# Expert blocks by quarters with VectorE block transposes and six weight transfers, in a hybrid SSD and mixture-of-experts layer

## What is computed

```python
logits = (xt @ router_w + router_b)
top_vals, top_idx = lax.top_k(logits, 4)
gates = softmax(top_vals)
# for every expert e, on the tokens that chose it:
gu  = xb @ w_gate_up[e] + b_gate_up[e]            # 1024 -> 2048
glu = minimum(gu[:, :1024], 7.0)
lin = clip(gu[:, 1024:], -7.0, 7.0)
act = glu * sigmoid(1.702 * glu) * (lin + 1.0)
y   = (act @ w_down[e] + b_down[e]) * gate        # 1024 -> 1024
out[token] += y
```

## Time and profile before

| | us |
|---|---|
| timed runs, median of 3 | 1688.03 (1685.74 to 1691.02) |
| profiled execution | 1686.66 |
| its span, first to last instruction | 1685.1 |
| PE busy | 1593.7 (95%) |
| DVE busy | 530.4 (31%) |
| ACT busy | 399.5 (24%) |
| POOL busy | 123.4 (7%) |
| bytes read from device memory | 470.4 MB |

### The profile page before, as it was taken

One profiled execution on the slowest core, in us unless ns is written; L12 is line 12 of the kernel. 1 busy time (PEld: TensorE's weight loads), 2 busy tenths in 40 slices (PEclk: granted clock), 3 DMA queues, 4 the chain that ended last, 5 costly groups with the idle time before them and its releaser, 6 DMA issues.

```text
span 1685.1 us, 42907 instructions
## 1 busy us (share of the span) xinstructions
PE 1593.7 (95%) x18227; PEld 1166.3 (69%) x18227; DVE 530.4 (31%) x893; ACT 399.5 (24%) x587; POOL 123.4 (7%) x211
## 2 busy tenths in 40 slices
PE   6898999999994999999999999999999999999992
PEld 4897888874443776777677776777677776777660
DVE  5666888863222111111211121111211121111117
ACT  5443333341121111211221111211221111211221
POOL 1000000000032000000000000000000000000000
PEclk9997999999995999999999999999999999999995
DMA  3222222334262999999999999999999999999926
GB/s 112 90 78 82 101 100 100 149 149 184 84 202 84 375 384 370 384 385 383 382 376 376 379 388 376 382 380 393 367 387 378 382 382 378 390 382 385 374 96 255
DMA packets 75288, 479.59 MB, mean 285 GB/s; under 512 B 12128, under 2 KB 12576, under 8 KB 21122
## 3 DMA queue, kind: packets, MB, share of 16 engines
q1 hardware_dynamic: 66258, 461.65, 71.2%
q0 software_dynamic: 9008, 17.65, 3.4%
HBM read 470.40 MB, written 17.37 MB: 289 GB/s over the span
## 4 chain that ended last, share of the span: by engine, by line
PE 66%; DVE 1%; issue 1%; DMA 0%; POOL 0%; ACT 0%; POOLq 0%; SPq 0%; DVEq 0%
PE bank L1433 21%; PE bank L1439 19%; PE bank L1455 13%; PE bank L1458 7%; PE bank L1471 2%; PE bank L1479 2%; PE bank L1410 2%; PE bank L1504 1%; DVE reg_b L1161 1%; DVE reg_x L1161 0%; DMA moe_f<-n_scratch,idx_next 0%; POOL slot_table L504 0%; DVE reg_x L1178 0%; DVE reg_b L1178 0%; DMA reg_x<-in_b_down 0%
## 5 line engine op out<-in xcount | busy, mean ns | idle before, releaser
L1439 PE MATMUL bank<-ring,moe_f 128*32 128x256 f32 (+1 forms) x4096 | 679.2, 327 | 0.0
L1433 PE MATMUL bank<-ring,moe_f 128*32 128x384 f32 x6144 | 675.0, 488 | 0.0
L1439 PEld LDWEIGHTS bank<-ring,moe_f 128*32 128x32 f32 x4096 | 444.2, 110 | 94.7 <-issue 0.5
L1458 PE MATMUL bank<-ring,moe_f 128*32 128x256 f32 x1536 | 343.5, 380 | 0.0
L1455 PE MATMUL bank<-ring,moe_f 128*32 128x512 f32 (+1 forms) x3072 | 343.1, 487 | 0.0
L1131 DVE TENSOR_SCALAR moe_f<-bank 128x384 f32<-128x384 f32 x64 | 35.7, 558 | 899.2 <-PE bank L1439 899.2
L1433 PEld LDWEIGHTS bank<-ring,moe_f 128*32 128x32 f32 x6144 | 246.6, 110 | 39.6 <-issue 14.0
L1191 PE MATMUL bank<-n_hi,w_hi 128*128 128x264 f32 (+2 forms) x640 | 199.5, 312 | 7.2 <-DVE w_lo L782 6.6
L1458 PEld LDWEIGHTS bank<-ring,moe_f 128*32 128x32 f32 x1536 | 163.7, 110 | 54.2
L1191 PE MATMUL bank<-n_lo,w_hi 128*128 128x264 f32 (+2 forms) x640 | 196.6, 307 | 0.0
L1191 PE MATMUL bank<-n_hi,w_lo 128*128 128x264 f32 (+2 forms) x640 | 196.3, 307 | 0.0
(11 more groups left out here) (229 smaller groups left out, 1188.9 us busy)
## 6 DMA issues: line engine op xcount, KB each, us to landing
ring<-in_moe SPq DMA_DIRECT2D x384, 1024.0 KB, 7.1
ring<-in_w_in SPq DMA_DIRECT2D x24, 1024.0 KB, 4.9
ring<-in_w_out SPq DMA_DIRECT2D x10, 1024.0 KB, 4.9
ring<-acs_scratch SPq DMA_DIRECT2D x4, 1024.0 KB, 6.7
ring<-expert_rows SPq DMA_DIRECT2D x4, 1024.0 KB, 6.7
ring<-expert_rows SPq DMA_DIRECT2D x2, 2048.0 KB, 14.0
reg_vcs<-in_xT SPq DMA_DIRECT2D x4, 528.0 KB, 6.9
reg_x<-in_xrow SPq DMA_DIRECT2D x4, 512.0 KB, 6.1
```

The lines of the kernel that those rows point to most:

```text
L1433: mm(bank[t * LANE:(t + 1) * LANE, 2 * h + k, 0:OWN], xT[:, c, t * LANE:(t + 1) * LANE], w[:, k * OWN:(k + 1) * OWN], start=False, stop=la ...
L1439: ins = mm(out[:, :, lo - k * BANK_FF:hi - k * BANK_FF], xT[:, c, t * LANE:(t + 1) * LANE], shared[:, :, lo - t * SHARED:hi - t * SHARED], ...
L1458: ins = mm(bank[3 * LANE:, 4 + k, t % 2 * Y_SHARED:(t % 2 + 1) * Y_SHARED], act(t), w[:, Y_OWN:], start=first and t != 1, stop=last, skip_ ...
```

## The change

The expert part is laid out another way.

- Lanes: lane l now takes quarter l (256 columns) of every chunk, for all 96 tokens, in three groups of 32 (`lanes` on PE). All matmuls are 256 columns wide, 12 per chunk. The weights are reordered on the host to match, also along the contraction dimension.
- x is gathered with token parts on all 128 partitions: three gathers, each of 128 rows of 1 KB (a quarter of a token's row per lane). The result is scattered the same way, three times 128 rows of 1 KB. The table's 96 rows are read by four small loads, one per lane, and POOL adds the lane's number to them.
- The transposes of x and of gate and up are VectorE block transposes (32x32 blocks); those on PE are gone, and so are their copies.
- The biases aren't matmuls. DVE adds them in the clips, block by block of 32 columns, with the bias as a scalar per partition taken at an address from a register (`bias_col`): four instructions of 128x96 for gate and four for up, per half. The split of the biases ahead of the loop is gone; they are loaded once, 256 KB.
- y is evicted by one copy, at the end of its own block, and scattered in the same turn of POOL's loop.
- Weights move in six transfers of 2 MB per block, 16 KB per partition. SP waits until both pieces of a pair have been used; PE waits once per pair.

The diff, cut to its core:

```diff
@@ sync
             def pieces(j, e):
-                for q in range(PIECES):
+                for q in range(0, PIECES, 2):
                     hold(piece_used, j * PIECES + (q + 2 - PIECES))
-                    sp.dma_start(slot(q), moe_d[ds(e, 1), q].rearrange("o p w -> (o p) w")).then_inc(w_in[q], 16)
+                    sp.dma_start(two_slots(q), moe_d[ds(e, 1), q // 2].rearrange("o p w -> (o p) w")).then_inc(w_in[q], 16)
...
@@ gpsimd
+            def list_rows(base):
+                for l in range(LANES):
+                    pool.dma_start(idx_raw[l * LANE:(l + 1) * LANE, :],
+                                   table_d[ds(base, BLOCK), :].rearrange("(r g) t -> r (g t)", g=GRANULES)).then_inc(idx_in, 16)
+            def lane_rows():
+                return g.tensor_tensor(idx_next[:, :], idx_raw[:, :], lane_off[:, :], ALU.add)
             def gather():
-                g.indirect_dma_start(out=xg[0:BLOCK, :], out_offset=None, in_=n2_d,
...
+                for n in range(GRANULES):
+                    g.indirect_dma_start(out=xg[:, n, :], out_offset=None, in_=n2_parts,
...
             with pool.Fori(0, n_blocks) as j:
                 base = pool.value_load(blocks[0:1, ds(2 * j + 2, 1)], min_val=0, max_val=EXPERTS * CAPACITY - BLOCK)
-                pool.dma_start(idx_next[0:BLOCK, :], table_d[ds(base, BLOCK), :]).then_inc(idx_in, 16)
-                hold((idx_in, j * 16 + 32), (xtr_done, j + 1))
+                list_rows(base)
+                hold((idx_in, j * (16 * LANES) + 32 * LANES))
+                lane_rows().then_inc(idx_moved, 1)
+                hold((idx_moved, j * 2 + 3), (xT_ready, j + 1))
                 gather()
                 hold((y_ready, j + 1))
                 scatter()
-                hold((y_out, j * 16 + 16), (x_in, j * 16 + 32))
+                hold((y_out, j * (16 * GRANULES) + 16 * GRANULES), (x_in, j * (16 * GRANULES) + 32 * GRANULES))
                 pool.sem_inc(y_room, 1)
...
@@ scalar
             with act.Fori(0, n_blocks) as j:
-                y_evict(j + 1)
                 for h in range(2):
                     act.wait_ge(glu_ready, j * 2 + h + 1)
                     a.activation(sig, glu, ACT.Sigmoid, scale=ALPHA).then_inc(sig_ready, 1)
...
+                act.wait_ge(piece_used, j * PIECES + PIECES)
+                act.wait_ge(y_room, j + 1)
+                a.copy(y_sb.rearrange("p g x -> p (g x)"), bank[:, 4:6, :].rearrange("p a b -> p (a b)")[:, 0:GRANULES * QUARTER]
+                       ).then_inc(y_ready, 1)
+                act.sem_inc(y_free_moe, 1)
...
@@ vector
+                    v.transpose(glu.rearrange("p b (g r) -> p g b r", g=GRANULES), gate).then_inc(gate_raw, 1)
+                    dve.wait_ge(gate_raw, j * 2 + h + 1)
+                    for b in range(FF_BLOCKS):
+                        ins = v.tensor_scalar(glu[:, b, :], glu[:, b, :], bias_col(0, b), LIMIT, ALU.add, ALU.min)
+                    ins.then_inc(glu_ready, 1)
+                    v.transpose(up.rearrange("p b (g r) -> p g b r", g=GRANULES), lin).then_inc(gu_free, 1)
                     dve.wait_ge(gu_free, j * 2 + h + 3)
-                    steps.done(v.scalar_tensor_tensor(lin, lin, 1.0, glu, ALU.add, ALU.mult))
+                    for b in range(FF_BLOCKS):
+                        ins = v.tensor_scalar(up[:, b, :], up[:, b, :], bias_col(1, b), 1.0 - LIMIT, ALU.add, ALU.max)
+                    ins.then_inc(up_ready, 1)
+                    dve.wait_ge(up_ready, j * 2 + h + 1)
+                    dve.wait_ge(glu_ready, j * 2 + h + 1)
+                    v.scalar_tensor_tensor(up, up, 1.0 + LIMIT, glu, ALU.min, ALU.mult).then_inc(lin_ready, 1)
...
                 swiglu(0)
                 swiglu(1)
                 x_transposed(j + 2)
...
@@ tensor
+                def lanes(b, x, at, w, first, last):
+                    out = bank[:, b:b + 2, :].rearrange("p a b -> p (a b)")
+                    for g in range(GRANULES):
+                        for l in range(LANES):
+                            ins = mm(out[l * LANE:(l + 1) * LANE, g * QUARTER:(g + 1) * QUARTER],
+                                     x[:, at, g * LANE:(g + 1) * LANE], w[:, l * QUARTER:(l + 1) * QUARTER],
+                                     start=first and g != 1, stop=last, skip_group_check=True)
+                    return ins
...
+                pe.wait_ge(xT_ready, j + 1)
+                pe.wait_ge(gu_free, j * 2 + 1)
+                for q in range(4):
+                    piece(q)
                 pe.wait_ge(gu_free, j * 2 + 2)
-                for b in range(4):
-                    mm(bank[:, b, 0:OWN], sel[:, :], bias_r[:, b * OWN:(b + 1) * OWN], start=True, stop=False,
-                       skip_group_check=True)
-                for q in range(6):
+                for q in range(4, GU):
                     piece(q)
...
+                pe.wait_ge(y_free_moe, j + 1)
+                pe.wait_ge(act_ready, j * 2 + 1)
                 piece(8)
                 piece(9)
+                pe.wait_ge(act_ready, j * 2 + 2)
                 piece(10)
                 piece(11)
```

More of the change, by code:

```diff
@@ L387, in _ @@
                 wout(r, WOUT_SLOT[r])
[L388 to L389 removed]
             sp.wait_ge(tile_done, TD_C + KC)
[L391 to L392 removed]
+            for q in range(SLOTS, PIECES, 2):
+                sp.dma_start(two_slots(q), moe_d[0, q // 2]).then_inc(w_in[q], 16)
             for m in range(TT):
@@ L403, in _ @@
                             wout(n, n)
-                        else:
-                            q = n % SLOTS
-                            sp.dma_start(slot(q), moe_d[0, q]).then_inc(w_in[q], 16)
+                        elif n % 2:
+                            q = (n - 1) % SLOTS
+                            sp.dma_start(two_slots(q), moe_d[0, q // 2]).then_inc(w_in[q], 16)
+            sp.dma_start(bias, bgu_d).then_inc(bias_in, 16)
             sp.wait_ge(list_ready, 1)
@@ new lines, in scatter @@
+            def scatter():
+                for n in range(GRANULES):
+                    g.indirect_dma_start(out=yk_parts, in_=y_sb[:, n, :], in_offset=None,
+                                         out_offset=bass.IndirectOffsetOnAxis(
+                                             ap=idx_now[:, 2 * n + 1:2 * n + 2].bitcast(U32), axis=0),
+                                         bounds_check=TOPK * SEQ * LANES - 1, oob_is_err=False).then_inc(y_out, 16)
+            list_rows(0)
+            pool.wait_ge(lane_ready, LANES)
@@ L1106, in _ @@
             dve.sem_inc(gm_ready, 1)
-            def choose_bias(e):
-                v.tensor_scalar(sel[:, :], sel_lane[:, :], sel_of[:, ds(e, 1)], None, ALU.mult).then_inc(sel_ready, 1)
             def x_transposed(n):
-                dve.wait_ge(xtr_done, n)
-                for half in (1, 0):
-                    v.tensor_copy(xT[:, 4 * half:4 * half + 4, :].rearrange("p c t -> p (c t)"),
-                                  bank[:, 6 + half, 0:4 * BLOCK]).then_inc(xT_ready, 1)
+                dve.wait_ge(x_in, n * (16 * GRANULES))
+                v.transpose(xT.rearrange("p b (g r) -> p g b r", g=GRANULES),
+                            xg.rearrange("p g (b r) -> p g b r", r=LANE)).then_inc(xT_ready, 1)
             dve.sem_inc(gu_free, 2)
-            steps.settled()
-            choose_bias(0)
+            dve.wait_ge(bias_in, 16)
+            up_bias = bias.rearrange("p (n k b) -> p n k b", k=2, b=FF_BLOCKS)[:, :, 1, :]
+            v.tensor_scalar(up_bias, up_bias, 1.0, None, ALU.add).then_inc(bias_ready, 1)
             x_transposed(1)
+            dve.wait_ge(bias_ready, 1)
             dve.wait_ge(list_in, 16)
@@ L1136, in swiglu @@
                     dve.wait_ge(sig_ready, j * 2 + h + 1)
-                    v.tensor_tensor(actv, lin, sig, ALU.mult).then_inc(act_ready, 1)
+                    v.tensor_tensor(act_h[h], up, sig, ALU.mult).then_inc(act_ready, 1)
                 swiglu(0)
-                e = dve.value_load(blocks[0:1, ds(2 * j + 3, 1)], min_val=0, max_val=EXPERTS - 1)
-                choose_bias(e)
                 swiglu(1)
                 x_transposed(j + 2)
-                steps.leave(n_blocks)
             for m in range(TT):
@@ L1460, in down @@
                     return ins
                 def piece(q):
-                    pe.wait_ge(w_in[q], j * 16 + 16 * (HELD[q] + 1))
+                    if q % 2 == 0:
+                        pe.wait_ge(w_in[q], j * 16 + 16 * (HELD[q] + 1))
                     for u in range(2):
-                        ins = gate_up(q, u) if q < GU else down(q, u)
-                    ins.then_inc(piece_used, 1)
-                def act_transposes(h):
-                    pe.wait_ge(act_ready, j * 2 + h + 1)
-                    for c in range(3):
-                        ins = nc.tensor.transpose(bank[:, 6 + h, c * P:(c + 1) * P],
-                                                  actv.rearrange("p a f -> p (a f)")[:, c * P:(c + 1) * P], ident[:, :])
```

(10 more changed lines are left out.)

228 lines of the change are left out of this document (61 added, 167 removed).

## The result

The change made the kernel slower: 1710.98 us (median of four runs, 1706.48 to 1712.27) against 1687.51 us (1685.74 to 1691.02), a ratio of 1.0132 with a 95% interval of 1.0107 to 1.0156. Forecast was 1651 us.

The account below looks back on a forecast made before the run. PE's order bounds the loop; after the change the largest of POOL's round (33.2 us a block), DMA (32.8) and PE (31.9) counts. 1686.7 - 40 + 2.3 + 0.5 = 1649.5, on the median's footing 1651 us; range 1590 to 1770.

Parts of the forecast that it names:

- PE per block, and the clips: Expert block on PE: streams 30.96 us, 3.50 us of changeovers gone, clip stall 0 to 1.9, middle 0.9: 31.9 us.
- DMA load: Expert block's transfers: weights 29.5 us at 426 GB/s plus 3.3 for POOL's small packets, 32.8 us (31.2 to 36.3).
- POOL's round: Expert loop, y's copy through scatter, lists, gather to transposed x: sets the period at 33.2 us, bounds 31.0 to 35.7.
- C = 33.5 us ... I take 34.5: Length C of POOL's round: terms sum to 33.5 us, 39.5 if small packets cost like 4 KB ones; 34.5 taken.
- P = (B + C) / 2: Block period P: round C must fit in two periods less PE's own part B; (31.9 + 34.5) / 2 = 33.2 us.
- That rival: Slower: POOL's small packets stand behind 16 KB weight rows in the DMA engines; C = 45, P = 38.45, 1819 us; chance 0.26.
- the case that I gave 0.26: Slower rival, small packets behind 16 KB rows in POOL's round: holds all times from 1693 us up; chance 0.26.
- B's kinder value: B is PE's own part of a block in the period formula; the forecast took 31.9 us.
- Ahead of the loop: Before the expert loop: more list loads, offsets and gathers, less for transposes, copies and bias matmuls; net +2.3 us.
- Behind it: After the loop: fewer eviction copies, two more scatter issues, reads of y start 1.4 us later; +0.5 us, up to +1.4.
- The signs I named: At a block's start, PE waiting for DVE's x transpose means the round, for weights the load; before piece 10, the clips.
- the slow case: Slower rival, small packets behind 16 KB rows; signs: period over 34.5 us; a gather landing after 14 us or more; chance 0.26.

Follow-up runs that it names:

- the lists ahead: The changed kernel, six 2 MB transfers kept, with POOL's four list loads for a block issued one turn earlier, ahead of the wait for y: 1582.45 us, ratio 0.9383.

## Why the prediction was wrong

*PE per block, and the clips.* Right in mechanism, and better than the 31.9 us I took: a block that doesn't wait is 31.08 us. The 3.50 us of changeovers are gone, the form of rows 3 is kept up for all chunks, and the clips never make PE wait. DVE's chain in the kernel after:

```profile
1006.72 0.58 DVE L1106 STREAM_TRANSPOSE moe_f<-bank 128x384 f32<-128x384 f32 x1 [14.51 <-PE bank L1400]
1007.48 0.81 DVE L1109 TENSOR_SCALAR moe_f<-moe_f 128x96 f32<-128x96 f32 x4 [0.17 <-DVE moe_f L1106]
...
1010.38 0.56 DVE L1121 TENSOR_TENSOR moe_f<-moe_f 128x384 f32<-128x384 f32 x1
```

1006.72 to 1010.94 is 4.2 us, against 5.15 us of cover. The 0.28 us of register issue per clip that I feared is not paid: four clips are done in 0.81 us.

*DMA load.* Mis-sized, without consequence: 32.8 us was too much, 31.3 is what 419 GB/s with all of POOL's traffic give. I had asked whether small packets cost the weights' rate; over the 29.5 us of the weights alone they add 1.8 us, close to the 1.7 us that I had put for their bytes. I had also read the engines' share of 0.99 at 381 GB/s as nearly full. It was no sign of it: the share is 1.02 at 393 GB/s in the kernel with 4 KB rows, where nobody waits for weights, and 1.01 at 419 with the lists ahead.

The 358 GB/s that the Trainium skill gives for a core's loads ("DMA: Bandwidth & Descriptors", "Where 436 GB/s comes from") is passed by 17% here, with one core running.

*POOL's round.* This is the step that failed, "C = 33.5 us ... I take 34.5". The mechanism was right: the round decides, and P = (B + C) / 2 holds. From the mean of 35.25 less the clock's 1.22, P = 34.03, so C = 2 x 34.03 - 31.08 = 37.0 us. It was the landings that I took from rows 6, which are those beside packets of 8 KB, for a kernel with packets of 16 KB. Term by term, mine against the median round after: scatter 9.1 and 10.6, lists with add 8.4 and 9.9, gather 10.6 and 11.1. With 8 KB rows they are 8.8, 8.2 and 9.0, less than mine: no price for four times as many small packets is seen beyond their issue, and the row length costs 1.8, 1.7 and 2.1 us, 5.5 us in all. I had seen this and put it in a rival, with 10.5 us for it and 6 for the packets. That rival had the mechanism (the experiments show it) and twice its price; it gave 1819 us. The measured 1711 us lies in the case that I gave 0.26, and inside my range of 1590 to 1770 us; the middle of the forecast, faster by 37 us, had the wrong sign.

As to how: "DMA: Bandwidth & Descriptors", "Queues, rings and completion order", of the Trainium skill says that each DMA engine takes turns between its queues packet by packet; its packet is a bundle of several descriptors, while a packet of the profile here is one row. A small packet would then wait for one bundle of large rows each turn, and longer by the length of the rows. The round agrees from 8 to 16 KB, and does not from 4 to 8 KB, where it stays at 30.8 us. No run shows the turns themselves, so how the row lengthens the landing is argued; that it does is shown.

*The missing term.* No step of the prediction had PE's clock in it, in the sum or in a rival. With C = 37.0 alone the period would by the same sum be 34.03 us, still under the 34.46 us of before, and the kernel at 1711 - 38 = 1673 us would be faster than before by 0.8%. The 2.5 us of half clock behind each of 15 stalls turn this to 1.3% slower. So the 60 us between forecast and result are: +26 us for the round (0.83 us x 31, B's kinder value included), +38 us for the clock, and -4 us for both ends.

*Ahead of the loop.* I had +2.3; from the end of the slot table's writes to the first weight matmul it is 14.6 us against 14.7. The gather's last part lands 2.75 us behind its issue, not 4.1, and so pays for the two issues more. The 1.5 us come from the table's writes, which end 1.4 us sooner (521.53 against 522.92 us); why is not shown. *Behind it*, +0.2 us where I had +0.5.

*The signs I named.* PE waited for DVE's x transpose and for nothing else: the round, as I had put it. The landing of 14 us that I gave as the mark of the slow case was far too high a mark; 8.4 in place of 6 us is enough when three of them stand in a row.

## What to carry to other kernels

Where a chain of small DMAs decides a period, price its landings by the packets that will run beside it, not by those of today; and look at the row length of the bulk transfer, not at its size: 2 MB in rows of 8 KB cost what 1 MB in rows of 8 KB did. A gain in rate from larger rows and transfers (415 to 419 GB/s here, 8 us, of which 2.3 are ahead of the first copy of y) is only to be had once the small chain is off the critical path, so move the chain first (lists a turn earlier: 1582 us from 1711). And add to a forecast stall of PE of the lengths seen here (3 to 7 us) the half clock behind it, 1.6 to 2.5 us: around break-even that decides the sign.

## What the runs showed that I had not expected

- One transfer of 64 neighbouring partitions in 16 KB rows: 230 GB/s, with the DMA engines' share at 1.01, where 128 partitions give 419. With the even and the odd 64 in turn PE no longer waited for weights, at the 369 GB/s that its blocks asked for.
- With PE asking for 421 GB/s, 1 MB pieces in 8 KB rows got 415 and 2 MB pieces in 16 KB rows 419. 4 KB rows carried the 393 that were asked of them.
- On one chip PE ran at half pace, at full granted clock, around the third issue of each of POOL's gathers, 1.0 to 1.4 us of matmuls each time; the traces from the others never show it.
- Useless matmuls made a kernel faster twice (by 18 and by 27 us), by keeping the granted clock at 1.00.
- A wait of 3.0 us in each block was enough for the clock to fall to 0.50, 1.4 us after PE had started again.
